# Early mixers: difference rows squared ahead of a step's maxima, one bias product for two

## The chip, the cores and the metric
One core of a Trainium2 chip runs the whole program. The metric is the device time of one execution in microseconds (us). The engines are TensorE (PE, with PEld for its weight loads), VectorE (DVE), ScalarE (ACT) and SyncE (SP), which issues the weight loads.

## The reference, cut to what matters
The program is a first block of two layers (hybrid mixer, dense or expert feed-forward, layer embedding) and a second block of two layers. The change is in the hybrid mixer of the first block, which runs once in each of its two layers. There, for 256 tokens:

```
qa, ka, va, qb, kb, vb, fb, qc, kc, vc, gc = split(xn @ w_in)
# difference attention: 8 softmax heads, 4 pairs
o   = causal_attention(qa, ka, va)
o_a = rmsnorm(o[:, :, 0] - lam * o[:, :, 1], subln_g) * (1 - lam_init)
# fox attention: 4 heads with a forget bias
log_f = log_sigmoid(fb + b_forget); cum = cumsum(log_f)
s[t, s'] = q[t] . k[s'] * scale + cum[t] - cum[s']     # then causal mask and softmax over s'
# retention: 4 heads, rotary on q and k, then group norm and silu gate
return concat(o_a, o_b, o_c) @ w_out
```

The term cum[t] is the same for every s' of a row, so the softmax over s' has the same value with or without it.

## The kernel before, in words
All work of an engine runs in one order written out by hand, and the engines wait for each other on counting semaphores. Weights come in pieces of 1 MB by SP into 7 raw slots. Each piece is rounded by ACT into a high part (`high`, 1.9 us) and DVE subtracts that for a low part (`low`, 2.3 us, L1684); PE multiplies with three products for each block (L676 to L678). Parts have three slots. `splits(done)` does the pieces up to three past the one named.

`attention1(l)` is written once for PE, once for ACT, once for DVE. It goes through steps i = 0 to 11, one head in each (`RUN1`): 0 to 7 are the difference heads, 8 to 11 the fox heads. On PE, step i does: `scores(i)`, the transposes `turn(i - 1)` (L774), the values product `values(i - 2)` (L783), and then half a projection of w_in (va, vfb, qkb, qkc, vgc, steps 0 to 9). In step 10 it transposes the rotated qc and kc instead; in steps 11 and 12 it does the retention scores (L883, L884) and values (L891 to L894). `scores` writes for two token tiles the product of q and k (L759), for a fox head the bias in two products against a one-hot column of the identity (L762 for cum[t], L763 for -cum[s']), and the causal mask (L765).

DVE in step i takes projected rows, then the row maxima of head i (`maxima`, L1852), then in steps 4, 6, 8 and 10 takes a finished pair of difference heads out of PSUM: reciprocal, scaling by lambda, two products (L1887 to L1891) into `ya` and `second`. Then the low parts of its piece. Step 6 has the chain of the forget gate, with two requests to ACT; step 8 the rotation of qc and kc (L2010 to L2015). At the end of step 10 DVE subtracts `second` from `ya` (L1914) and sums the squares (`squares_of`, L1991, L1992). After step 11 it requests the square root (`rstd_ask`, L1728), weighs two heads of retention scores (`weigh`, L1919), waits for the root (`rstd_answer`, L1733), applies root and gain (`gained`, L1985, L1987) and marks the rows ready (`mark`, L1711).

ACT in step i does the exponentials of head i (L1368) once their maxima are there, copies the turned probabilities of head i - 1 (L1378), and the high part of its piece. In step 10 it first copies the vgc rows (L1392, L1394), in step 11 first the transposed qc and kc (`take`, L1357), for which the retention scores wait. Its Sqrt for the difference rows (`serve_sqrt(8)`, L1284) comes after step 11. ACT changes its table of functions (ACT_TABLE_LOAD) between Exp and Sqrt; Copy needs none.

After this `mixed(l)` transposes the rows of all three parts (L647) and multiplies with w_out; these are the dense rows that begin at 158.68 us in layer 0.

Of the kernel before, what the change touches and what calls it, by code (L numbers as in the profile page):

```python
# [24 lines left out]
ALU = mybir.AluOpType  # L25
# [3 lines left out]
P = 128  # L29
# [9 lines left out]
HEADS4 = 4  # L39
# [81 lines left out]
def program(nc, io, out, cut=99):  # L121
    ctx = ExitStack()
    with ctx:
# [367 lines left out]
        def tok(i):  # L491
            return slice(i * P, (i + 1) * P)
# [142 lines left out]
        def _(pe):  # L635
# [113 lines left out]
            def scores(name, u, g):  # L749

                if g >= 2:
                    pe.wait_ge(att_exp, g - 1)
                q, k, _ = att_operands(name, u)
                for t, (c0, n) in enumerate(att_shape(name)[2]):
                    if name == "memory":
                        last = pe.matmul(bank[g % 2][:, c0:c0 + n], q[:, tok(t)], k[:, 0:n], start=True, stop=True)
                        continue
                    dst = bank[g % 2][:, c0:c0 + n]
                    pe.matmul(dst, q[:, tok(t)], k[:, 0:n], start=True, stop=False)  # L759
                    if name == "fox":  # L760
                        one = ident[0:HEADS4, u:u + 1]
                        pe.matmul(dst, fox[:, 2, tok(t)], one.to_broadcast([HEADS4, n]), start=False, stop=False)  # L762
                        pe.matmul(dst, one.to_broadcast([HEADS4, P]), fox[:, 3, 0:n], start=False, stop=False)  # L763

                    last = pe.matmul(dst[:, t * P:(t + 1) * P], ident_one[:, :], causal[:, :], start=False, stop=True)  # L765
                last.then_inc(att_scores, 1)
# [487 lines left out]
        def _(act):  # L1254
# [125 lines left out]
            def attention1(l):  # L1380

                first = att_first["diff", l]
                for i in range(len(RUN1) + 1):
                    if i == 2:
                        act.wait_ge(xn_ready, norm_no["mix", l] + 1)
                        for t in range(NT):
                            take(("va", l, t), v[:, t, 0:512], rst[:, t:t + 1])
                    if i == 10:
                        act.wait_ge(rotated, l + 1)
                        for t in range(NT):  # L1390
                            filled(act, ("vgc", l, t))
                            act.activation(sg[:, t, :], bank_of(("vgc", l, t))[:, 256:512], ACT.Copy,  # L1392
                                           scale=rst[:, t:t + 1])
                            act.activation(v[:, t, 768:1024], bank_of(("vgc", l, t))[:, 0:256], ACT.Copy,  # L1394
                                           scale=rst[:, t:t + 1]).then_inc(unit_act, 1)
                    if i == 11:
                        take(("qcT", l), flat(qT, 6, 2))
                        take(("kcT", l), flat(kT, 6, 2))
                    if i < len(RUN1):
                        exps(*RUN1[i], first + i)  # L1400
                    if i == 12:
                        serve_sqrt(8)
                    if i >= 1:
                        copy_turned(RUN1[i - 1][0], first + i - 1)
                    if i == 6:
                        serve(fox[:, 1, :], fox[:, 1, :], ACT.Exp, scale=-1.0)
                        serve(fox[:, 1, :], fox[:, 1, :], ACT.Ln, bias=1.0)
                    if 1 <= i <= 10:
                        splits(pieces_of[("va", "vfb", "qkb", "qkc", "vgc")[(i - 1) // 2], l][(i - 1) % 2])
                    if (l, i) == (0, 1):  # L1410
                        serve(stat[:, 1, 0:2 * LAYERS], stat[:, 0, 0:2 * LAYERS], ACT.Exp)
# [264 lines left out]
        def _(dve):  # L1676
# [178 lines left out]
            def attention1(l):  # L1855
# [4 lines left out]
                for i in range(len(RUN1)):  # L1860
                    if i == 4:
                        for t in range(NT):
                            key = ("vfb", l, t)
                            filled(dve, key)
                            dve.tensor_scalar(forget_rows[:, t, :], bank_of(key)[:, 256:260], rst[:, t:t + 1], None,
                                              ALU.mult)
                            dve.tensor_scalar(v[:, t, 512:768], bank_of(key)[:, 0:256], rst[:, t:t + 1], None,
                                              ALU.mult).then_inc(unit_dve, 1)
                    if i == 5:
                        take_scaled(("qkb", l, 0), qT[:, 4:6, :], 0.125)  # L1870
                    if i == 6:
                        key = ("forgetT", l)
                        filled(dve, key)
                        dve.tensor_scalar(fox[:, 0, :], bank_of(key)[0:HEADS4, 0:SEQ], bforget[:, l:l + 1], None,
                                          ALU.add).then_inc(unit_dve, 1)
                        take_scaled(("qkb", l, 1), kT[:, 4:6, :])
                    if i == 8:
                        for t in range(NT):
                            filled(dve, ("qkc", l, t))
                            dve.tensor_scalar(a1[:, t * G:(t + 1) * G], bank_of(("qkc", l, t))[:, :], rst[:, t:t + 1],  # L1880
                                              None, ALU.mult).then_inc(unit_dve, 1)
                    maxima(*RUN1[i], first + i)
                    if i in (4, 6, 8, 10):
                        hd = (i - 4) // 2
                        dve.wait_ge(att_pv, first + i - 2)
                        r = rinv[:, 4 * hd:4 * hd + 4]
                        link(dve.reciprocal(r, rowsum[:, 4 * hd:4 * hd + 4]))  # L1887
                        link(dve.tensor_scalar(r[:, 2:4], r[:, 2:4], lam[:, l:l + 1], None, ALU.mult))
                        o = bank[4 + hd % 2][:, :].rearrange("p (n t d) -> p n t d", n=2, t=NT)
                        dve.tensor_tensor(ya[:, :, hd, :], o[:, 0], per(r[:, 0:2], P), ALU.mult)  # L1890
                        dve.tensor_tensor(second[:, :, hd, :], o[:, 1], per(r[:, 2:4], P),  # L1891
                                          ALU.mult).then_inc(out_taken, 1)
                    if i == 6:
                        emptied(dve, ("forgetT", l))
                        link(dve.tensor_scalar(fox[:, 1, :], fox[:, 0, :], -1.0, None, ALU.mult))
                        ask(dve.tensor_tensor(fox[:, 1, :], fox[:, 1, :], fox[:, 0, :], ALU.max))
                        ask(dve.tensor_scalar(fox[:, 0, :], fox[:, 0, :], 0.0, None, ALU.min))
                        link(dve.tensor_tensor(fox[:, 0, :], fox[:, 0, :], fox[:, 1, :], ALU.subtract))
                        link(dve.memset(fox[:, 1, :], 1.0))
                        link(dve.tensor_tensor_scan(fox[:, 2, :], fox[:, 1, :], fox[:, 0, :], 0.0, ALU.mult, ALU.add))  # L1900
                        dve.tensor_scalar(fox[:, 3, :], fox[:, 2, :], -1.0, None, ALU.mult).then_inc(cum_ready, 1)
                    if 1 <= i <= 10:
                        splits(pieces_of[("va", "vfb", "qkb", "qkc", "vgc")[(i - 1) // 2], l][(i - 1) % 2])
                    if (l, i) == (0, 1):
                        setup_lambda()
                    if i == 8:
                        emptied(dve, ("qkc", l, 1))
                        rotate(a1[:, :].rearrange("p (t h n) -> p t h n", t=NT, h=8), 8, 0, 32, rot,
                               a2[:, :].rearrange("p (t h n) -> p t h n", t=NT, h=8),
                               [flat(qT, 6, 2), flat(kT, 6, 2),  # L1910
                                sg[:, :, :].rearrange("p t n -> p (t n)")]).then_inc(rotated, 1)
                    if i == 10:
                        dve.wait_ge(out_taken, out_use["diff", l, 3] + 1)
                        link(dve.tensor_tensor(ya, ya, second, ALU.subtract))  # L1914
                        squares_of(ya, 4, P)

                def weigh(u):
                    dve.wait_ge(ret_scores, HEADS4 * l + u + 1)
                    dve.tensor_tensor(ret_w[:, u, :], bank[6 + u % 2][:, 0:3 * P], decay[:, u, :],  # L1919
                                      ALU.mult).then_inc(ret_weights, 1)  # L1920

                rstd_ask(rinv[:, 0:8], 8, 1.0 / P)
                weigh(0)
                weigh(1)
                rstd_answer(8)
                link(gained(ya, 4, P, g_subln[:, l, :]))
                mark().then_inc(y_ready, 1)
                weigh(2)
                weigh(3)
                dve.wait_ge(att_pv, first + len(RUN1))  # L1930
# [585 lines left out]
```

## Time and profile before

| | |
|---|---|
| median of 3 runs | 2122.72 us (2120.93 to 2123.65) |
| the profiled execution's own time | 2124.18 us |
| its span, first to last instruction | 2122.4 us |
| busy share PE, DVE, ACT | 95%, 73%, 58% |
| granted clock of PE, mean | 0.970 |
| HBM traffic | 502 MB read, 237 GB/s over the span |

The busy share is a mean over stages that have different limits; the mixer's attention takes some 110 us in each of the two layers of 2122. A granted clock of 1.00 is 2.4 GHz, 0.50 is 1.2 GHz. In timelines the number in brackets is the time the engine stood idle before an instruction, with what ended it. Starts of following instructions of one engine can lie closer than their durations, since they overlap.

### The profile page before, as it was taken

What the parts mean: (1) busy time and instruction counts of PE and PEld (TensorE: products, weight loads), DVE (VectorE), ACT (ScalarE), POOL (GpSimd) and SP (SyncE); (2) the same over time, 40 slices, a digit from 0 to 9 for tenths busy, and PEclk for the clock granted to TensorE, in tenths of its full rate; (3) what the DMA queues carried; (4) which work ended last, traced back from release to release, by engine and by line L of the source; (5) the groups of instructions that cost most, each with busy time, mean ns of one, the idle gap of its engine ahead of it and who ended that gap; (6) DMA issues with size and microseconds to landing.
All of it is one profiled execution on the core that took longest, in us unless ns stands there. A gap on an engine that the chain in (4) does not pass through costs nothing.

```text
span 2122.4 us, 27418 instructions
## 1 busy us (share of the span) xinstructions
PE 2026.0 (95%) x10545; PEld 1711.3 (81%) x10545; DVE 1554.2 (73%) x1526; ACT 1234.5 (58%) x1300; POOL 0.2 (0%) x4
## 2 busy tenths in 40 slices
PE   5999999999899999999999999999988999999998
PEld 5878999887778888888888888888877887878886
DVE  4455555646579898988988898888885855866575
ACT  4434434644467777777777777777776545254532
POOL 0000000000000000000000000000000000000000
PEclk8978999999899999999999999999998999999999
DMA  8414555450479999999999999999975542335320
GB/s 269 161 60 144 183 195 190 130 178 1 168 256 378 334 370 345 358 375 329 375 331 368 347 355 377 328 374 334 369 275 176 179 145 74 126 137 194 119 71 29
DMA packets 242709, 504.47 MB, mean 238 GB/s; under 512 B 11321, under 2 KB 58681, under 8 KB 242617
## 3 DMA queue, kind: packets, MB, share of 16 engines
q1 hardware_dynamic: 242328, 503.10, 66.8%
q8 instruction: 63, 1.03, 0.2%
q14 instruction: 30, 0.24, 0.0%
q10 hardware_dynamic: 288, 0.11, 0.0%
HBM read 502.12 MB, written 1.05 MB: 237 GB/s over the span
## 4 chain that ended last, share of the span: by engine, by line
PE 86%; DVE 7%; ACT 3%; issue 2%; SPq 2%; DMA 0%; DVEq 0%; ACTq 0%
PE bank L676 25%; PE bank L678 25%; PE bank L677 25%; DVE low L1684 2%; PE bank L759 2%; PE bank L1086 1%; PE bank L783 1%; PE bank L1044 1%; ACT high L1264 1%; PE bank L647 1%; SPq L627 1%; PE bank L774 1%; PE bank L1173 1%; ACT high L1440 1%; SPq L591 1%
## 5 line engine op out<-in xcount | busy, mean ns | idle before, releaser
L2238 DVE TENSOR_TENSOR low<-raw,high 128x2048 fp32r<-128x2048 f32 x336 | 768.3, 2291 | 107.1 <-ACT high L1440 106.4
L1440 ACT ACTIVATE high<-raw 128x2048 fp32r<-128x2048 f32 x336 | 644.7, 1919 | 249.8 <-PE bank L678 247.9
L1684 DVE TENSOR_TENSOR low<-raw,high 128x2048 fp32r<-128x2048 f32 (+1 forms) x139 | 312.8, 2260 | 174.9 <-ACT high L1264 174.4
L1264 ACT ACTIVATE high<-raw 128x2048 fp32r<-128x2048 f32 (+1 forms) x139 | 262.9, 1896 | 178.4 <-PE bank L678 178.0
L676 PE MATMUL bank<-high,xg_hi 128*128 128x512 f32 x896 | 354.4, 396 | 2.5 <-DVE lone L2192 2.5
L678 PE MATMUL bank<-high,xg_lo 128*128 128x512 f32 x896 | 349.9, 391 | 0.0
L677 PE MATMUL bank<-low,xg_hi 128*128 128x512 f32 x896 | 349.3, 390 | 0.0
L676 PE MATMUL bank<-high,xT_hi 128*128 128x512 f32 (+1 forms) x576 | 230.4, 400 | 5.6 <-DVE xT_lo L1700 1.8
L677 PE MATMUL bank<-low,xT_hi 128*128 128x512 f32 (+1 forms) x576 | 223.9, 389 | 0.0
L678 PE MATMUL bank<-high,xT_lo 128*128 128x512 f32 (+1 forms) x576 | 223.8, 388 | 0.0
L676 PE MATMUL bank<-high,hT_hi 128*128 128x512 f32 x536 | 210.1, 392 | 0.0
L677 PE MATMUL bank<-low,hT_hi 128*128 128x512 f32 x536 | 208.7, 389 | 0.0
L678 PE MATMUL bank<-high,hT_lo 128*128 128x512 f32 x536 | 208.7, 389 | 0.0
L676 PE MATMUL bank<-xT_hi,high 128*128 128x256 f32 x672 | 195.1, 290 | 11.0 <-DVE low L1684 5.0
L676 PEld LDWEIGHTS bank<-high,xg_hi 128*128 128x128 f32 x896 | 168.7, 188 | 36.6 <-DVE lone L2192 2.8
L678 PEld LDWEIGHTS bank<-high,xg_lo 128*128 128x128 f32 x896 | 168.5, 188 | 36.0
L677 PEld LDWEIGHTS bank<-low,xg_hi 128*128 128x128 f32 x896 | 168.9, 188 | 33.8
L677 PE MATMUL bank<-xT_lo,high 128*128 128x256 f32 x672 | 193.4, 288 | 0.0
L678 PE MATMUL bank<-xT_hi,low 128*128 128x256 f32 x672 | 193.1, 287 | 0.0
L676 PEld LDWEIGHTS bank<-xT_hi,high 128*128 128x128 f32 x672 | 132.1, 197 | 13.0 <-issue 5.3
L676 PEld LDWEIGHTS bank<-high,xT_hi 128*128 128x128 f32 x576 | 110.4, 192 | 28.8 <-issue 2.2
L677 PEld LDWEIGHTS bank<-xT_lo,high 128*128 128x128 f32 x672 | 132.2, 197 | 0.4
(311 smaller groups left out, 2435.3 us busy)
## 6 DMA issues: line engine op xcount, KB each, us to landing
raw<-in_moe_w_gate SPq DMA_DIRECT2D x112, 1024.0 KB, 5.5
raw<-in_moe_w_up SPq DMA_DIRECT2D x112, 1024.0 KB, 5.6
raw<-in_moe_w_down SPq DMA_DIRECT2D x112, 1024.0 KB, 5.5
raw<-in_w_in SPq DMA_DIRECT2D x64, 1024.0 KB, 5.4
raw<-in_w_out SPq DMA_DIRECT2D x20, 1024.0 KB, 4.9
raw<-in_dense_w_gate SPq DMA_DIRECT2D x11, 1024.0 KB, 5.3
raw<-in_dense_w_up SPq DMA_DIRECT2D x11, 1024.0 KB, 5.4
raw<-in_dense_w_down SPq DMA_DIRECT2D x11, 1024.0 KB, 4.9
```

What stands on the lines that cost most here:

```text
L591: sp.dma_start(raw[:, slot, 0:k * n].rearrange("p (k n) -> p k n", k=k), src).then_inc(landed[slot], 16)
L627: sp.dma_start(dst, source).then_inc(consts_in, 16)
L647: last = pe.transpose(bank_of(key)[:, (k * NT + t) * P:(k * NT + t + 1) * P], rows[:, t, (2 * j + k) * P:(2 * j + k + 1) * P], ident[:, :])
L676: pe.matmul(dst, stationary[0], moving[0], start=start, stop=False)
L677: pe.matmul(dst, stationary[0], moving[1], start=False, stop=False)
L678: return pe.matmul(dst, stationary[1], moving[0], start=False, stop=stop)
L759: pe.matmul(dst, q[:, tok(t)], k[:, 0:n], start=True, stop=False)
L774: last = pe.transpose(bank[2 + g % 2][:, b * P:(b + 1) * P], probs[:, g % 2, b * P:(b + 1) * P], ident[:, :])
L1264: act.activation(high[:, slot, 0:k * n], raw[:, raw_slot[piece], 0:k * n], ACT.Copy).then_inc(high_done, 1)
L1440: act.activation(high[:, k % PARTS, :], raw[:, slot, :], ACT.Copy).then_inc(s["high"], 1)
L1684: dve.tensor_tensor(low[:, slot, 0:k * n], src, high[:, slot, 0:k * n].bitcast(F32), ALU.subtract).then_inc(low_done, 1)
L2238: dve.tensor_tensor(low[:, k % PARTS, :], raw[:, at0 + k % slots, :], high[:, k % PARTS, :].bitcast(F32), ALU.subtract).then_inc(s["low"], 1)
```

## The change
Five edits, all in `scores` and the two `attention1` of ACT and DVE. The product of cum[t] (L762) is left out. On DVE the maxima of each step go behind the take-out of a pair (steps 4, 6, 8, 10); in step 10 the subtraction, the squares and the request for the root go ahead of the maxima, and the answer, root, gain and mark right behind them, where all of these stood after the low part of step 10 or after step 11. The low part of step 10 goes to step 11, behind its maxima. On ACT the Sqrt goes from step 12 to step 10, between the vgc copies and the exponentials.

```
@@ scores (PE)
                     pe.matmul(dst, q[:, tok(t)], k[:, 0:n], start=True, stop=False)
                     if name == "fox":
                         one = ident[0:HEADS4, u:u + 1]
-                        pe.matmul(dst, fox[:, 2, tok(t)], one.to_broadcast([HEADS4, n]), start=False, stop=False)
                         pe.matmul(dst, one.to_broadcast([HEADS4, P]), fox[:, 3, 0:n], start=False, stop=False)
@@ attention1 (ACT)
                             act.activation(v[:, t, 768:1024], bank_of(("vgc", l, t))[:, 0:256], ACT.Copy,
                                            scale=rst[:, t:t + 1]).then_inc(unit_act, 1)
+                        serve_sqrt(8)
                     if i == 11:
                         take(("qcT", l), flat(qT, 6, 2))
                         take(("kcT", l), flat(kT, 6, 2))
                     if i < len(RUN1):
                         exps(*RUN1[i], first + i)
-                    if i == 12:
-                        serve_sqrt(8)
@@ attention1 (DVE)
-                    maxima(*RUN1[i], first + i)
                     if i in (4, 6, 8, 10):
                         hd = (i - 4) // 2
...
                                           ALU.mult).then_inc(out_taken, 1)
+                    if i == 10:
+                        dve.wait_ge(out_taken, out_use["diff", l, 3] + 1)
+                        link(dve.tensor_tensor(ya, ya, second, ALU.subtract))
+                        squares_of(ya, 4, P)
+                        rstd_ask(rinv[:, 0:8], 8, 1.0 / P)
+                    maxima(*RUN1[i], first + i)
+                    if i == 10:
+                        rstd_answer(8)
+                        link(gained(ya, 4, P, g_subln[:, l, :]))
+                        mark().then_inc(y_ready, 1)
...
-                    if 1 <= i <= 10:
+                    if 1 <= i <= 9:
                         splits(pieces_of[("va", "vfb", "qkb", "qkc", "vgc")[(i - 1) // 2], l][(i - 1) % 2])
+                    if i == 11:
+                        splits(pieces_of["vgc", l][1])
...
-                    if i == 10:
-                        dve.wait_ge(out_taken, out_use["diff", l, 3] + 1)
-                        link(dve.tensor_tensor(ya, ya, second, ALU.subtract))
-                        squares_of(ya, 4, P)
...
-                rstd_ask(rinv[:, 0:8], 8, 1.0 / P)
                 weigh(0)
                 weigh(1)
-                rstd_answer(8)
-                link(gained(ya, 4, P, g_subln[:, l, :]))
-                mark().then_inc(y_ready, 1)
                 weigh(2)
                 weigh(3)
```

## Rows read from the trace of the kernel before

**Rows 1.** The page, part 4: shares of the span in the chain that ended last, by engine
```profile
PE 86%; DVE 7%; ACT 3%; issue 2%; SPq 2%; DMA 0%; DVEq 0%; ACTq 0%
```

**Rows 2.** PE's waits, layer 0, 50 to 165 us: us in total, times, longest
```profile
PE bank L774 <- ACT probs L1368: 4.0, 1, 4.0
```

**Rows 3.** The same of layer 1, 430 to 550 us
```profile
PE bank L774 <- ACT probs L1368: 4.2, 1, 4.2
```

**Rows 4.** The chain in order of time, layer 0: start, us, what
```profile
138.39 2.29 DVE low L1684
140.68 1.14 DVE yf L1914
...
141.85 1.24 DVE scr L1991
...
143.10 1.23 DVE rinv L1992
...
144.36 0.63 DVE negmax L1852 x2
...
145.98 0.90 PE bank L774 x3
```

**Rows 5.** Timeline of PE, layer 0: start, us, instruction
```profile
131.85 0.48 PE L762 MATMUL bank<-ident,yf 4*128 4x128 f32 x2
132.18 0.38 PE L763 MATMUL bank<-yf,ident 4*128 4x128 f32 x2
...
133.28 0.70 PE L762 MATMUL bank<-ident,yf 4*128 4x256 f32 x2
133.81 0.59 PE L763 MATMUL bank<-yf,ident 4*128 4x256 f32 x2
...
140.34 1.18 PE L883 MATMUL bank<-qT,kT 64*128 64x256 f32 x4
...
158.68 0.76 PE L676 MATMUL bank<-high,xT_hi 128*128 128x512 f32 x1 [0.73 <-issue]
```

**Rows 6.** Timeline of DVE, layer 0; in brackets the idle time before and its releaser
```profile
97.08 0.17 DVE L1887 RECIPROCAL rinv<-rowsum 128x4 f32<-128x4 f32 x1
...
98.22 0.27 DVE L1895 TENSOR_SCALAR yf<-yf 4x256 f32<-4x256 f32 x1
...
113.90 0.62 DVE L1852 TENSOR_REDUCE negmax<-bank 128x1 f32<-128x128 f32 x2 [1.34 <-PE bank L765]
...
127.66 2.29 DVE L1684 TENSOR_TENSOR low<-raw,high 128x2048 fp32r<-128x2048 f32 x1 [3.17 <-ACT high L1264]
```

**Rows 7.** Timeline of ACT, layer 0, step 10
```profile
135.26 0.37 ACT L1368 ACTIVATE probs<-bank,negmax 128x128 f32<-128x128 f32 x1 [2.08 <-DVE negmax L1852]
...
138.71 0.61 ACT L1357 ACTIVATE kT<-bank 128x512 f32<-128x512 f32 x1
```

**Rows 8.** Timeline of ACT, second attention, around its Sqrt
```profile
1729.72 1.28 ACT L1284 ACT_TABLE_LOAD   x1
...
1731.24 1.28 ACT L1368 ACT_TABLE_LOAD   x1
```

**Rows 9.** Timelines of DVE and PE, layer 1
```profile
499.81 0.62 DVE L1852 TENSOR_REDUCE negmax<-bank 128x1 f32<-128x128 f32 x2 [1.68 <-PE bank L765]
...
510.59 0.62 DVE L1852 TENSOR_REDUCE negmax<-bank 128x1 f32<-128x128 f32 x2 [0.72 <-PE bank L765]
514.38 2.29 DVE L1684 TENSOR_TENSOR low<-raw,high 128x2048 fp32r<-128x2048 f32 x1 [3.17 <-ACT high L1264]
...
525.84 0.98 PE L883 MATMUL bank<-qT,kT 64*128 64x256 f32 x4
...
531.49 0.90 PE L774 MATMUL bank<-ident,probs 128*128 128x128 f32 x3 [4.24 <-ACT probs L1368]
```

**Rows 10.** Stretches: length, busy PE, PEld, DVE, ACT, POOL; PEclk, DMA share, GB/s
```profile
123.50:126.50 3.00, 3.00 (x13) 2.71 (x12) 0.99 (x3) 1.98 (x6) 0.00 (x0) 0.50 0.37 125
...
140.50:164.00 23.50, 18.73 (x76) 16.27 (x77) 16.52 (x32) 5.82 (x14) 0.00 (x0) 0.50 0.00 0
```

## The prediction

> **What bounds the kernel now.** I read four views. First the page's chain of waits: TensorE (PE) holds 86% of the chain that ended last [rows 1], so a microsecond counts where PE idles for another engine, or where PE itself has less to do with nothing else late. Second, PE's waits in the two attention stretches: each has one large wait, 4.0 us in layer 0 and 4.2 us in layer 1, of the last fox head's transposes (L774) for its exponentials [rows 2, 3]. Third, the chain in order of time shows what stands in that wait: the low part of a weight piece (L1684), subtraction, squares and their sum (L1914, L1991, L1992), then the maxima of the last step (L1852), then exponentials [rows 4]. The difference rows, 3.7 us of VectorE (DVE) work, stand ahead of maxima that PE waits for. Fourth, the timelines of PE, DVE and ScalarE (ACT) [rows 5 to 7, 9], from which the new order can be laid out. I number the steps i = 0 to 11 as the code does; steps 8 to 11 are the fox heads.
>
> **The bias product (L762).** It goes 16 times, 8 in each layer. By starts, one for the first token tile takes 132.18 - 131.85 = 0.33 us of PE and one for the second 133.81 - 133.28 = 0.53 us [rows 5], so a head saves 0.86 us, a layer 3.4 us, both 6.9 us. Whether it shortens anything depends on what is late next.
>
> **The out-take block (L1887 to L1891) now stands ahead of the maxima of steps 4, 6, 8 and 10.** From its start to the next instruction it takes 98.22 - 97.08 = 1.14 us [rows 6]. The values product it waits for is that of head i - 3, which PE does in step i - 1 ahead of that step's projection, so the wait is over by then. In step 8 DVE idled 1.34 us in layer 0 and 1.68 us in layer 1 ahead of the maxima [rows 6, 9]: the block fits. In steps 4 and 6 it delays the maxima by up to 1.1 us; PE asks for those exponentials only a step later, some 5 us or more after the scores, and the fox gate chain of step 6 stood behind the same block before, so it gets at most some 0.15 us later. I take 0 on PE for these three steps and -0.1 us on the DVE chain that leaves step 8 of layer 0, because scores (8) are ready 0.86 us earlier, and DVE, not PE, is then the later. Step 9 follows at DVE's own pace, since the rotation fills it: in layer 0, low part (9) starts at 127.66 - 0.1 and the next DVE instruction can start 2.21 us later (its 2.29 us less an overlap of 0.08), so DVE is free at F = 129.77. In layer 1 the maxima of steps 8 and 9 did wait for PE, 1.68 us (of which the block uses 1.14) and 0.72 us [rows 9]; both shrink as scores come earlier, so this chain gains 0.54 + 0.72 = 1.25 us: F = 514.38 - 1.25 + 2.21 = 515.34.
>
> **Step 10, DVE.** From F: block with its link 1.25 us (1.14 plus 0.1 for the last instruction's end), then L1914, L1991, L1992 at 1.25 to 1.26 each by their starts [rows 4], 3.77: the request for the square root is issued at F + 5.0. Scores (10) are ready before that, so the maxima follow at once and end at F + 5.7. The subtraction used to be behind the low part of step 10; that low part moves behind the maxima of step 11, and no one is near needing it: its piece belongs to the output projection.
>
> **Step 10, ACT.** ACT now waits in its queue for that request, and exponentials (10), copy (9), the high part and the two copies of qc and kc are queued behind it. The Sqrt needs another activation table than Exp. The second attention has just this order: a table load of 1.28 us at 1729.72, the Sqrt, and the load back at 1731.24, 1.52 us after the first [rows 8]. I take the first load as put ahead of the wait, where ACT has 3 us of idle; it costs nothing there (without that cover, 1.28 us a layer). The load back is bare: a load and a Sqrt, 1.52 us by the starts of rows 8. With 0.2 from request to Sqrt, exponentials (10) start at F + 6.72. Before they started at 135.26, and kc's copy ended at 138.71 + 0.61 = 139.32, 4.06 us later [rows 7]; the instructions between are the same. So kc is there at F + 10.8, and the retention scores (L883), which wait for it, start at 140.57 instead of 140.34 in layer 0 and at 526.15 instead of 525.84 in layer 1 [rows 5, 9]. **PE's saving is thus all given back at this point**: it idles about 1.6 us ahead of transposes (10) and 2.2 us ahead of L883.
>
> The Trainium skill ("ScalarE: Activation LUTs", What ACT_TABLE_LOAD costs) puts a switch of table at 1.28 us plus a drain of 1.38 us. By the skill the load back would end 1.38 us later and the sum below would be 2.8 us smaller. The trace disagrees: 1.52 us hold the load of 1.28 us and the Sqrt, with no room for a drain [rows 8].
>
> **Step 11 and after.** L883 and L884 take 1.6 us (140.34 to the start of the idle, 145.98 - 4.04) [rows 2, 4, 5]. The gain rows (L1985, L1987) and the mark are done by F + 8.5, maxima (11) right behind, exponentials (11) on ACT at F + 10.8 to 11.7: all ahead of PE. Transposes (11) then start at 142.17, where they started at 145.98: **3.8 us earlier**; in layer 1 at 527.75 against 531.49 [rows 9]: **3.75 us**. The first retention weights are due 1.9 us later; the moved low part lets DVE go at F + 12.1, in time. From there to the output projection PE was busy throughout. The square root of the retention norm needs its own table load now; ACT idled 4 us ahead of it, so it is covered.
>
> PE's clock was at half (1.2 GHz, granted 0.50) from 140.5 to 164.0 us in layer 0 [rows 10], and for as long in layer 1; it fell before the wait of 4 us began, while PE did small products, and rose 5.3 us into the dense rows, which began at 158.68 [rows 5]. I leave that stretch as it is, merely 3.8 us shorter. The short fall inside the fox steps (123.5 to 126.5 [rows 10]) may go or stay; since DVE sets the pace there, it does not move the end. What is gained carries to the end: the expert stage waits for PE, not for transfers, and loads start when pieces are used.
>
> **Sum.** 3.8 + 3.75 = 7.5 us. The profiled execution took 2124.18 us, which makes 2116.7; the median of the runs is 1.46 us lower, so I forecast 2115.2 us. A measurement of this kernel can tell about 0.2%, 4.2 us, from no change.
>
> **Rivals.**
> *PE sets the pace after all.* If my DVE and ACT chain is too long, the two waits (8.2 us) and all products (6.9 us) go: 15.1 us, 2107.6. For it: PE's 86%. Against it: kc's copy cannot come before the square root in ACT's order. 10%.
> *The switch of table holds ACT a load's length longer*: the first load bare too, or ACT at a standstill around the second, 1.28 us more a layer, 2117.8. For it: in rows 8 the request had come before the load, so they don't show on which side of a pending wait it stands. Against it: their load back is bare of anything else. 14%. The Trainium skill's drain (same section) would be such a standstill.
> *The blocks of steps 4, 6 and 8 add up* instead of sinking into idle time: 3.4 us a layer on F, which leaves 0.4 us: 2122.0, no difference. Against it the idle time ahead of the maxima in rows 6 and 9. 12%.
> *The clock stays down* (the slower side). Place: the rows of the output projection. With the new idle pieces among small products PE could come to the dense rows needing longer to be given 2.4 GHz. Each microsecond of full speed work done at half costs one more; from 3.75 us of such work a layer the gain is gone, and if 8.6 us of the rows behind 164.0 were done at half, the time would be 2115.2 + 17.2 = 2132.4. Against it: the clock came back 5.3 us into the dense rows, which began at 158.68 [rows 5, 10] and are unchanged. 6%.
> The forecast itself has 58%.
>
> **Numbers.** The forecast's own range, with runs spread over 2.7 us and the clock's rise some 1.5 us earlier or later, is 2112 to 2118.5. The range of 8 in 10 takes in the bare load and most of the adding up: 2111 to 2121. The chance of faster by over 0.2% (below 2118.5): 0.58 less a little, 0.10 and over half of 0.14, 0.74; within 0.2%: 0.20; slower: 0.06.
>
> **What would show it.** PE's waits should show the 4 us wait on exponentials (11) gone, and in its place some 1.6 us ahead of transposes (10) and 2.2 us ahead of the retention scores, waiting for kc's copy, in each layer. ACT should show a load, Sqrt and load between its vgc copies and exponentials (10). L762's group should be gone with the other bias product left at 32 records. DVE should run from F without idle to maxima (10). I am wrong if the retention scores start over 1 us earlier or later against the end of the projections than laid out, or if the low clock outlasts the first 6 us of the dense rows.

## The result and the profile after

| | before | changed |
|---|---|---|
| median of the runs on one chip (4 each) | 2123.18 us (2120.93 to 2128.11) | 2109.07 us (2107.55 to 2113.32) |
| ratio, 95% interval | | 0.9939 [0.9919, 0.9959] |
| profiled execution: time, span, mean granted clock | 2124.18, 2122.4 us, 0.970 | 2113.32, 2111.5 us, 0.971 |
| PE's wait ahead of transposes (11), layer 0, layer 1 | 4.0, 4.2 us | 0, 0 us |
| forecast | | 2115.2 us (2111 to 2121) |

The sign is right. The time lies 6.1 us below the forecast and 1.9 us below the range. Of the runs behind the table of experiments, three took 4017, 6585 and 7007 us and are left out of every median, mean and ratio. The profile after, first the page's shares of the chain that ended last, against [rows 1]:

```profile
PE 81%; DVE 10%; ACT 5%; issue 2%; SPq 2%; DMA 0%; DVEq 0%; ACTq 0%
```

PE lost five points to DVE and ACT, on which more of the chain now lies. PE's waits in layer 0 (100 to 150 us), against [rows 2]; columns are us in total, times, longest:

```profile
PE bank L885 <- ACT kT L1359: 0.6, 1, 0.6
```

and in layer 1 (480 to 600 us), against [rows 3]:

```profile
PE bank L776 <- ACT probs L1370: 1.9, 1, 1.9
PE bank L885 <- ACT kT L1359: 1.1, 1, 1.1
```

The wait of 4 us is gone, and two smaller ones stand a step earlier, where the prediction had them. The chain in order of time, layer 0, against [rows 4] (start, us, what):

```profile
128.64 2.29 DVE low L1685
...
132.11 1.24 DVE yf L1895
...
133.37 1.24 DVE scr L1995
...
134.63 1.23 DVE rinv L1996
...
135.88 0.18 DVE stat L1729
...
136.31 1.28 ACT L1370
...
137.61 0.02 ACT probs L1370
...
141.19 0.49 ACT kT L1359
...
141.72 1.23 PE bank L885 x4
```

It is now one chain from the low piece to the retention scores: difference rows, request, load back, exponentials (10), kcT. From low (9) to exponentials (10) it takes 137.61 - 128.64 = 8.97 us; the working had 2.21 + 6.72 = 8.93. ACT's timeline beside it, against [rows 7, 8]:

```profile
131.68 1.28 ACT L1286 ACT_TABLE_LOAD   x1
136.09 0.21 ACT L1286 ACTIVATE stat<-stat 128x8 f32<-128x8 f32 x1 [3.12 <-DVE stat L1729]
136.31 1.28 ACT L1370 ACT_TABLE_LOAD   x1
137.61 0.37 ACT L1370 ACTIVATE probs<-bank,negmax 128x128 f32<-128x128 f32 x1
...
141.06 0.61 ACT L1359 ACTIVATE kT<-bank 128x512 f32<-128x512 f32 x1
```

The first load stands ahead of the pending wait (it ends at 132.96, the Sqrt goes at 136.09), so it is hidden; the load back is bare, with exponentials 0.02 us behind it. PE's timeline, layer 0, against [rows 5]:

```profile
130.35 0.48 PE L765 MATMUL bank<-yf,ident 4*128 4x128 f32 x2
130.76 0.23 PE L767 MATMUL bank<-causal,ident_one 128*128 128x128 bf16 x1
130.92 0.70 PE L759 MATMUL bank<-kT,qT 64*128 64x256 f32 x2
131.55 0.69 PE L765 MATMUL bank<-yf,ident 4*128 4x256 f32 x2
132.17 0.23 PE L767 MATMUL bank<-causal,ident_one 128*128 128x128 bf16 x1
...
143.31 0.90 PE L776 MATMUL bank<-ident,probs 128*128 128x128 f32 x3
```

A token tile's bias by starts now takes 130.76 - 130.35 = 0.41 us and 132.17 - 131.55 = 0.62 us. Transposes (11) start 143.31 - 128.64 = 14.67 us behind low (9), where before it was 145.98 - 127.66 = 18.32 us [rows 4, 6]: 3.65 us less behind that point, and the point itself comes earlier.

**Where the time went.** Against scores (4), transposes (11) start 4.1 us earlier in each layer, 8.2 us together, forecast 7.5. Of the 10.9 us between the two spans another 2.65 us come from the start of the dense stage, where the kernel before had TensorE at half clock (first line) and the changed one did not (second):

```profile
189.00:195.00 6.00, 5.92 (x27) 0.50 1.07 369
```

```profile
189.00:195.00 6.00, 6.00 (x53) 1.00 1.08 373
```

(Stretch, length, PE's busy time and instructions, PEclk, DMA share, GB/s.) The changed kernel's first step began 1.45 us late, and the rest, 1.5 us, is small shifts. The cause of that half clock is open. In the mixers' ends the low clock stayed. Windows of the changed kernel, against [rows 10], first its tail of layer 0, then the stretch in which the kernel before has its short fall:

```profile
133.20:159.60 26.40, 25.09 (x101) 20.68 (x101) 16.88 (x30) 9.83 (x21) 0.00 (x0) 0.50 0.00 1
```

```profile
122.00:127.00 5.00, 5.00 (x27) 1.00 0.68 210
```

The long fall lasts 26.4 us (23.5 before), the short one is gone. The long fall began at 133.2 us, while PE was busy, and ahead of its only wait in this stretch (141.1 to 141.7 us).

### The profile page after: what moved, and what is told of

It is laid out like the page before. It is cut to its first block, busy times and chain, and to the rows that moved or that the text cites. A ratio compares the mean times of both kernels' runs of the same rounds, so it can differ in the third digit from the quotient of the medians.

```text
span 2111.5 us, 27356 instructions
## 1 busy us (share of the span) xinstructions
PE 2019.1 (96%) x10513; PEld 1703.5 (81%) x10513; DVE 1553.0 (74%) x1526; ACT 1239.0 (59%) x1304; POOL 0.2 (0%) x4
## 4 chain that ended last, share of the span: by engine, by line
PE 81%; DVE 10%; ACT 5%; issue 2%; SPq 2%; DMA 0%; DVEq 0%; ACTq 0%
PE bank L676 24%; PE bank L678 24%; PE bank L677 24%; DVE low L1685 3%; ACT high L1266 2%; PE bank L1088 1%; PE bank L1046 1%; PE bank L785 1%; PE bank L759 1%; PE bank L647 1%; SPq L627 1%; ACT probs L1370 1%; PE bank L1175 1%; ACT high L1441 1%; SPq L591 1%
```

## Experiments

PE's tail below is the time from transposes (11) to the last turned rows of y, layer 0; "wait" is PE's wait ahead of transposes (11) alone, so a kernel with 0 there can still wait elsewhere. Mean clock is the mean over a kernel's runs. The ratio is to the runs of the kernel before on the same chip, which had, in the four comparisons, medians of 2118.27 (the first four rows), 2118.08 (late root, late root with step 10 only, copy, before again), 2117.01 (late root again, product back and the delays) and 2116.78 us (the last row), and mean clocks of 0.9713 or 0.9714.

| kernel | median us | ratio, 95% interval | mean clock | wait L0, L1 | tail |
|---|---|---|---|---|---|
| changed, again | 2108.43 | 0.9952 [0.9937, 0.9968] | 0.9742 | 0, 0 | 26.1 |
| product alone | 2113.18 | 0.9973 [0.9964, 0.9982] | 0.9736 | 5.4, 5.4 | 25.5 |
| order alone | 2115.38 | 0.9992 [0.9977, 1.0007] | 0.9711 | 0, 0 | 24.2 |
| step 10 only | 2112.04 | 0.9956 [0.9939, 0.9973] | 0.9736 | 0, 0 | 26.3 |
| late root | 2089.38 | 0.9861 [0.9840, 0.9882] | 0.9835 | 0, 0 | 20.5 |
| late root, again | 2091.92 | 0.9891 [0.9863, 0.9919] | 0.9805 | 0, 0 | 20.5 |
| late root, step 10 only | 2095.27 | 0.9904 [0.9871, 0.9936] | 0.9787 | 0, 0 | 20.5 |
| copy for the root | 2107.83 | 0.9943 [0.9924, 0.9962] | 0.9740 | 0, 0 | 26.2 |
| before, again | 2120.34 | 1.0007 [0.9994, 1.0020] | 0.9702 | 4.2, 4.2 | 26.9 |
| late root, product back | 2115.86 | 0.9984 [0.9970, 0.9999] | 0.9713 | 0, 0 | 26.5 |
| late root, delay of one | 2108.78 | 0.9959 [0.9945, 0.9974] | 0.9735 | 2.5, 2.5 | 27.0 |
| late root, delay of two | 2110.04 | 0.9964 [0.9951, 0.9977] | 0.9749 | 5.0, 5.0 | 25.6 |
| product and late root | 2102.49 | 0.9923 [0.9897, 0.9950] | 0.9775 | 1.3, 1.3 | 25.4 |

**The changed kernel again**, on the chip of the next three.

> The changed kernel itself, unchanged, run again to see how steady its gain is and how it goes with the granted clock. What the two traces show at matched places: the stretch from the fourth scores to the output projection is 4.1 us shorter in each layer, 8.2 us in all, where 7.5 were forecast; the rest of the 10.9 us between the profiled executions is half-clock time elsewhere. Theory A (the rest is chance in when the clock falls): 8 to 9 us faster than before once executions of the same mean clock are compared, and 8 to 14 as medians fall. Theory B (the change itself makes the clock fall less often): again 12 to 14 us faster, and the mean clock of all its executions 0.002 or more above the kernel before. Theory C (layout or another lasting cause outside the mixers): 12 to 14 us faster at equal clock.

2108.43 us, ratio 0.9952: 9.8 us faster on this chip. That size is between theory A's 8 to 9 and the 12 to 14 of B and C, and the interval reaches from 6.8 to 13.3 us; the mean clock lies 0.0029 above the kernel before, the sign that theory B names. Its trace shows the waits of layer 0 whole:

```profile
PE bank L776 <- ACT probs L1370: 1.9, 1, 1.9
PE bank L885 <- ACT kT L1359: 1.8, 1, 1.8
```

3.7 us; the prediction had 1.6 + 2.2 = 3.8. In the first trace PE's clock had already fallen at 133.2, its small products took longer, and they covered 3.1 us of the same waits; the retention scores started at the same point of DVE's chain both times. Layer 1 has 1.9 + 1.1 = 3.0 us in both traces: there the clock fell during the first wait, and the slower products behind it covered 0.7 us of the second.

**The product alone**: the kernel before without the query's product.

```
-                        pe.matmul(dst, fox[:, 2, tok(t)], one.to_broadcast([HEADS4, n]), start=False, stop=False)
```

> The kernel before with the product of cum[t] (L762) left out and nothing moved. Theory A (the chain through VectorE and ScalarE sets the pace in step 9 and 10, as laid out): in the order of before, scores (10) are late for VectorE by 4.65 us in layer 0 and 3.44 us in layer 1, so all three products ahead of it count, 3 x 0.86 = 2.6 us a layer, and the fourth is swallowed by the 4 us wait: 5.2 us faster, the waits of TensorE on the last exponentials stay at 4.0 us plus 0.86. Theory B (fewer falls of the clock): the short fall in a fox step, 3 us at half in each layer, is gone too: 7 to 8.5 us faster with a higher mean clock. Rival (additive): 6.9 us and the waits shrink by none.

5.1 us faster, by the interval 3.8 to 7.6, so the time alone can't tell theory A's 5.2 from the additive rival's 6.9. The wait ahead of transposes (11) grew from 4.0 to 5.4 us, so PE's own saving is partly given back to it, as a chain paced by DVE makes it. Yet the trace gains 3.6 us a layer from scores (4) to transposes (11), 7.2 us in all, nearer to theory B. The starts of scores (8), (9) and (10) stand 9.54 and 11.17 us apart before, 8.88 and 8.87 us here: 0.66 us a step for the product, and 1.6 us for a short fall of the clock that is not there any more.

**The order alone**: the changed kernel with the query's product back.

```
                         one = ident[0:HEADS4, u:u + 1]
+                        pe.matmul(dst, fox[:, 2, tok(t)], one.to_broadcast([HEADS4, n]), start=False, stop=False)
```

> The changed kernel with the product of cum[t] put back, so only the order of VectorE and ScalarE differs from before. Theory A: the retention scores start at F + 10.8 with F = 129.95 and 516.67, that is 0.4 and 1.6 us later than before, and the last transposes 3.6 and 2.5 us earlier: 6.1 us faster. With the product alone at 5.2 the two don't add up to more than the change because the product's time is lost in front of the copy of kc: sum 11.3 against 8.2. Rival (additive): change minus product, 13 - 6.9 = 6 us, and product alone 6.9, so that the sum is the change. Theory B: as A, and the mean clock like that of before, 0.970, as the long fox steps are back.

2.9 us faster by the medians, 0.9992 [0.9977, 1.0007]: not told from no change, where theory A had 6.1 us. PE waits for no other engine in the mixer's end of either layer, and still the retention scores of layer 0 start 1.7 us later than before, counted from scores (4), and those of layer 1 3.6 us later. Transposes (11) start 2.4 and 0.4 us earlier, where theory A had 3.6 and 2.5. Two windows of this kernel show why:

```profile
117.00:122.00 5.00, 5.00 (x18) 0.68 0.22 74
...
127.00:132.00 5.00, 5.00 (x22) 0.66 0.00 1
```

Both steps, 8 to 9 and 9 to 10, take 11.14 us; the kernel before has one such fall. In layer 1 the long fall comes early, at some 513 us:

```profile
510.00:520.00 10.00, 10.00 (x41) 0.64 0.00 0
```

(the kernel before: 1.00 in this window, and at half only from some 526 us). The wait was exchanged for work at half clock. So product and order are worth 5.1 and 2.9 us alone and 9.8 together by the medians, each good to some 2 to 3 us.

**Step 10 only**: the changed kernel with the maxima ahead of the scaling rows in steps 4, 6 and 8.

```
+                    if i != 10:
+                        maxima(*RUN1[i], first + i)
                     if i in (4, 6, 8, 10):
...
-                    maxima(*RUN1[i], first + i)
                     if i == 10:
+                        maxima(*RUN1[i], first + i)
```

> The changed kernel with the maxima of steps 4, 6 and 8 ahead of the take-out of a pair again; step 10 stays as changed. Theory A (those three moves cost and bring nothing on TensorE): equal to the changed kernel within 1 us; VectorE's step 8 starts its maxima as soon as scores (8) are there, up to 0.9 us earlier, so the last transposes come up to 0.9 us earlier in each layer if the chain through VectorE is the bound: 0 to 1.8 us faster than the changed kernel. Rival (the moves ahead matter by themselves): slower than the changed kernel by over 2 us.

The intervals overlap almost wholly, 0.9956 against 0.9952; in the traces its transposes (11) come 0.2 us a layer earlier against scores (4). So in the traces the blocks of steps 4, 6 and 8 cost 0.2 us a layer, which the times can't show.

**The late root.** The waits of 1.9 and 1.8 us are the price of asking for the root ahead of exponentials (10). This kernel keeps the scaling rows first, but lets the difference rows follow the maxima, answers the root after two retention weighings, and has ACT serve it in step 12.

```
+                    maxima(*RUN1[i], first + i)
                     if i == 10:
                         dve.wait_ge(out_taken, out_use["diff", l, 3] + 1)
                         link(dve.tensor_tensor(ya, ya, second, ALU.subtract))
                         squares_of(ya, 4, P)
                         rstd_ask(rinv[:, 0:8], 8, 1.0 / P)
-                    maxima(*RUN1[i], first + i)
-                    if i == 10:
-                        rstd_answer(8)
-                        link(gained(ya, 4, P, g_subln[:, l, :]))
-                        mark().then_inc(y_ready, 1)
...
                 weigh(1)
+                rstd_answer(8)
+                link(gained(ya, 4, P, g_subln[:, l, :]))
+                mark().then_inc(y_ready, 1)
                 weigh(2)
```

> The changed kernel with the two pieces of its step 10 put apart: the scaling rows still run ahead of step 10's maxima, but subtraction, squares and sums come behind those maxima, and the root is asked for there and answered only between the second and third retention weighing, with the vector engine's last low piece after step 11's maxima; the scalar engine serves the root in step 12 again. Theory A (in the changed kernel step 10's exponentials wait for 3.7 us of difference rows, for the root and for two table loads): without these exponentials start some 5 us earlier after the block, the copy of kcT stands at step 10's scores + 7.0 us instead of + 11.1, retention's first scores at + 7.6 instead of + 11.8, and the transposes of step 11 at + 9.2 instead of + 13.4 us: 4.2 us a layer, some 8 us in all, so about 2101 us where the changed kernel has 2109, ratio to the kernel before about 0.992. Rival (the difference rows only change places: they come late for the turned rows y at the end of the mixer, as in the kernel before, so TensorE waits there instead): the transposes of step 11 come earlier by 4 us and the first turned y row does not; the time stays within 1 us of the changed kernel.

2089.38 us: theory A had 2101, and the gain over the changed kernel is 19 us instead of 8 (the two ran on different chips; their ratios, 0.9861 and 0.9952, say the same). PE's timeline in layer 0:

```profile
129.07 0.49 PE L759 MATMUL bank<-kT,qT 64*128 64x128 f32 x2
...
136.65 0.71 PE L885 MATMUL bank<-qT,kT 64*128 64x256 f32 x4
...
137.57 0.55 PE L776 MATMUL bank<-ident,probs 128*128 128x128 f32 x3
```

Scores (10) to the retention scores: 7.58 us, to transposes (11): 8.50 us (9.2 expected, 13.4 in the changed kernel). That is 4.9 us a layer. Another 5.8 us a layer stand behind transposes (11): the tail takes 20.5 us instead of 26.3, because the clock no longer falls (130 to 165 us, the changed kernel 0.61):

```profile
130.00:165.00 35.00, 32.84 (x190) 1.00 0.00 1
```

The changed kernel's transposes of 0.90 us take 0.55 us here. Neither theory had this part. PE is not without waits here. The retention weights come late twice in each layer, and the clock stays at 1.00 through it:

```profile
PE bank L893 <- DVE ret_w L1924: 1.0, 2, 0.6
```

**The late root with step 10 only**: steps 4, 6 and 8 as in the kernel before.

> The kernel with the late root, and in steps 4, 6 and 8 the maxima ahead of the scaling rows as in the kernel before; only step 10 keeps the rows first. Theory A: as the step-10-only kernel stood to the changed one in their traces, 0.2 us a layer earlier, 0.4 us in all, which the times can't tell; the same time as the kernel with the late root. Rival (the order in steps 4, 6 and 8 matters by the clock, which falls where TensorE works on little): over 1 us to either side.

Its trace is that of the late root to 0.1 us up to the dense stage, but its six runs reach from 2088.2 to 2110.2 us, with mean clocks from 0.986 down to 0.971. The median lies 5.9 us above the late root's on this chip and 3.4 us above its repeat; the ratios' intervals overlap with both, so neither theory A nor the rival is settled by the times.

**A copy in place of the root** (no table changes in step 10; the kernel leaves the square root out).

```
-                        serve_sqrt(8)
+                        serve(stat[:, 1, 0:8], stat[:, 0, 0:8], ACT.Copy)
```

> The changed kernel, where the scalar engine answers the request of step 10 with a copy instead of the root (this leaves the root out of the normalised rows of the first mixer, in both layers), so neither its table load nor the load back to the exponentials' table takes place. Theory A (the load back, 1.28 us, stands between the answer and step 10's exponentials; the load ahead is hidden in the wait): step 10's exponentials start some 1.0 to 1.3 us earlier, TensorE's waits of 0.6 us (layer 0) and 1.1 us (layer 1) on kcT go, 1.7 us in all, up to 2.5 us if the later scores of layer 1 also move up. Rival (nothing waits on it: TensorE has other work): below 0.5 us.

ACT's timeline, layer 0:

```profile
134.12 0.21 ACT L1286 ACTIVATE stat<-stat 128x8 f32<-128x8 f32 x1 [4.45 <-DVE stat L1729]
134.64 0.37 ACT L1370 ACTIVATE probs<-bank,negmax 128x128 f32<-128x128 f32 x1 [0.32 <-DVE negmax L1853]
```

Exponentials (10) start 0.52 us after the answer instead of 1.52; the maxima are then the later by 0.32. From scores (10) to transposes (11) it takes 12.42 us instead of 13.38 and 13.37: 0.95 us a layer, 1.9 us together, theory A's size. The waits for kcT, which theory A had go, stay at 1.9 and 1.1 us; it is the wait of 1.9 us ahead of transposes (10) that shrinks to 1.0. The times, 2107.83 against 2108.43, on different chips, can't show it.

**The kernel before again**, as a kernel of its own.

> The kernel before, unchanged, against itself: how far apart two medians of it come, and a second trace of it. Theory A (the three runs that the prediction started from lay high, and most of the miss comes from there): its own median is 2117.5 to 2119.5 us, not 2122.7, and the two stand at 1.000 within 0.001. Theory B (the short falls of TensorE's clock in the mixers' last steps belong to this order of instructions): its trace shows one of them, some 1.6 us long, between the scores of step 9 and of step 10 in each layer again. Rival to B: they fall in other steps, or in none.

1.0007 [0.9994, 1.0020], but 2.3 us apart in the medians: 2120.34 us (12 runs) and 2118.08 us (17). Theory A's bound of 2119.5 us is passed; its second half, 1.000 within 0.001, holds. All five later medians of this kernel do lie 2.4 to 5.9 us below the 2122.72 us of the first three runs. The second trace has one short fall in each layer too, in layer 0 a step earlier, in layer 1 again between scores (8) and (9); so the rival to theory B holds for layer 0:

```profile
112.00:117.00 5.00, 5.00 (x21) 0.66 0.64 206
```

It also has the half clock at the start of the dense stage. Which step it falls in differs between the traces; that it falls once is the same in both traces and both layers.

**The product back, and two delays**, all from the late root: what holds the clock?

```
+                        pe.matmul(dst, fox[:, 2, tok(t)], one.to_broadcast([HEADS4, n]), start=False, stop=False)
```

> The kernel with the late root, with the query's part of the forget bias added by its own product again in each fox head: the kernel before but for the order of step 10 and of the root. Theory A (what brought 20 us below the changed kernel is TensorE's clock, which stays at full in the end of the mixers when step 11's transposes don't wait; the product isn't needed for that): 4 x 0.66 = 2.6 us a layer back, and a short fall of the clock of 1.6 us a layer in the steps 8 to 10 as in the traces of the kernel before; 6 to 9 us above the kernel with the late root, 2095 to 2098 us, ratio to before 0.988 to 0.990. Rival (the product belongs to what holds the clock): the clock falls again at the end of the mixers, 12 us more, 2107 to 2111 us.

24 us slower than the late root on the same chip, for 5.3 us of products: the rival's direction, and 5 us beyond its range. PE waits for no other engine in its tail, and its clock falls at some 134 us all the same:

```profile
130.00:135.00 5.00, 5.00 (x24) 0.90 0.00 0
135.00:140.00 5.00, 5.00 (x22) 0.50 0.00 0
```

The delays do squares and sums of the difference rows twice, or three times, ahead of maxima (11):

```
-                        squares_of(ya, 4, P)
+                        for again in range(2):
+                            squares_of(ya, 4, P)
```

> The kernel with the late root, with squares and sums of the difference rows done twice over (the second time changes nothing), ahead of step 11's maxima: 2.5 us of work more on the vector engine at a place where its exponentials have some 0.15 us to spare, so TensorE's transposes of step 11 wait about 2.3 us in each layer. Theory A (a wait there lets the clock fall until the projection after the mixer is well under way): 2.3 us of waiting and some 6 us of half clock a layer, 16 us in all, about 2105 us. Rival (a wait costs itself alone): 4.6 us, about 2094 us.

> The same with squares and sums done three times over: 5.0 us more on the vector engine, a wait of about 4.8 us a layer. Theory A: 4.8 us of waiting and 6 us of half clock a layer, about 2111 us; the step from no delay to one (16 us) is larger than the step from one to two (5 us). Rival (a wait costs itself alone): 9.6 us, about 2099 us, both steps the same.

With one, the wait is 2.5 us in each layer:

```profile
PE bank L776 <- ACT probs L1370: 2.5, 1, 2.5
```

```profile
135.00:140.00 5.00, 2.50 (x24) 1.00 0.00 0
140.00:145.00 5.00, 4.45 (x24) 0.60 0.01 3
```

and the time 2108.78, 16.9 us above the late root of the same chip (16 expected; 4.6 by the rival). PE idles at full clock, and the fall comes behind the wait. With two, the wait is 5.0 us, the time 2110.04: 1.3 us more, not 5. Theory A's shape holds, its second step is too large; the tail shrinks from 27.0 to 25.6 us, and the two intervals overlap. Here the fall comes inside the wait, which ends at 143.69 us:

```profile
140.00:145.00 5.00, 1.31 (x7) 0.72 0.00 0
```

**The late root again**, beside these three.

> The kernel with the late root once more, on the chip of its three variants: 2089 us and a mean clock of 0.983 again if its gain belongs to the kernel; a spread as wide as that of its sister with step 10 alone (2088 to 2110 us) if it is a chance of each execution whether the clock holds in both mixers.

2091.92 us, and the trace the same in the tail; its six runs reach from 2082.8 to 2102.5 us, clocks from 0.986 to 0.974. Both expectations are half right: the gain belongs to the kernel, and how much of it a run gets is partly chance.

**Product and late root, without the change's order of the scaling rows.**

```
+                    maxima(*RUN1[i], first + i)
                     if i in (4, 6, 8, 10):
...
-                    maxima(*RUN1[i], first + i)
                     if i == 10:
```

> The kernel with the late root, with the scaling rows behind the maxima again in steps 4, 6, 8 and 10, as in the kernel before: of the change only the product is left, and the late root stands on it. By the trace of the kernel with the late root, the 1.2 us of scaling rows then stand between step 10's maxima and the difference rows, step 11's maxima come 1.2 us later, and step 11's transposes wait about 1.1 us in each layer, between none (late root) and 2.5 us (delay of one). Theory A (the order of the scaling rows is worth nothing but this wait, and the clock holds through it): 2.2 us above the kernel with the late root, 2091 to 2096 us. Rival (a wait of 1.1 us is enough for the clock to fall): 2104 to 2109 us, as with the delay of one; then the change's order is what makes the gain of the late root possible.

PE waits 1.3 us in each layer:

```profile
PE bank L776 <- ACT probs L1370: 1.3, 1, 1.3
```

```profile
135.00:140.00 5.00, 3.22 (x27) 1.00 0.00 0
140.00:145.00 5.00, 4.97 (x24) 0.53 0.01 3
```

and the clock falls in this trace in both layers. The median is 2102.49 us, the runs from 2093.9 to 2110.1: between the two forecasts, neither holds. The spread suggests that a wait of 1.3 us makes the fall likelier, not certain; only one execution has a trace. The scaling rows' place is worth 7 to 13 us here by the ratios (0.9923 against the late root's 0.9891 and 0.9861, each on its own chip); its interval overlaps with that of the late root's repeat, so the size is rough.

## Why the prediction was off

**Right.** The chain on DVE and ACT, to 0.04 us from low (9) to exponentials (10); the first table load hidden and the load back bare, with no drain; the waits' new places and their sum (3.7 against 3.8 us in layer 0 of the second trace; 3.0 us in layer 1 of both, where the clock fell in between); the moved low piece free; the blocks of steps 4, 6 and 8 sunk into idle time, but for 0.2 us a layer; PE's own saving given back: 4.1 us a layer where 3.8 and 3.75 were laid out.

**The steps that failed.**

1. *"the median of the runs is 1.46 us lower, so I forecast 2115.2 us"*. The base of three runs lay high: later medians of the same kernel are 2116.8 to 2120.3 us. A forecast of -7.5 us is a ratio of 0.9965, outside the first comparison's [0.9919, 0.9959] and just inside the second's [0.9937, 0.9968]. From the base of that second chip, 2118.27 us, it reads 2110.8 us, 2.3 us above what was measured there. So 4.5 us of the 6.1 us is the base, and the range took this spread too lightly. Whether the first runs lay high by chance, or something lasting about that chip raised the kernel before alone, no run tells: the changed kernel had 2109.07 us there and 2108.43 us on the second. The first comparison's 14.1 us between the medians contain that high base too; 9.8 us is the better figure for the change.
2. *"a head saves 0.86 us"*. It is 0.66: the kept product lost its overlap, 0.41 and 0.62 us by starts where they were (with the two together) 0.33 and 0.53 us for the removed one alone. The sum went by DVE's chain, so this changed nothing in it.
3. *"The short fall inside the fox steps may go or stay; since DVE sets the pace there, it does not move the end."* It went: in all 22 mixers traced without the product (11 traces of 9 kernels) scores (8), (9) and (10) stand 8.87 or 8.88 us apart, while of the eight traced with it six have falls in these steps. And it did move the end a little: low (9) starts 50.10 us behind scores (4) instead of 50.57 in layer 0, and 50.02 instead of 51.67 in layer 1, 0.47 and 1.65 us earlier, where 0.1 and 1.25 were laid out. That is about the 0.7 us that the two layers gained over the forecast. Which part of it the fall gave, and which the product, was not taken apart.
4. *"I leave that stretch as it is"*. For this change it held, as the change left waits of 3.0 to 3.7 us a layer. This stretch held the larger prize, some 6 us a layer, and no case priced it. The half clock at the start of the dense stage, 2.65 us in both traces of the kernel before and in neither of the changed one, was not seen either; kernels with and without the product show it, so its cause stays open, and with it some 1.6 us of the miss.

**The rivals.** PE setting the pace (2107.6) came out close in time but not in mechanism: 3.0 to 3.7 us of waits a layer remained. The table switch and the adding up are refuted by the timelines. The clock staying down (the slower side) did not occur; its opposite was what mattered. The order alone came nearest to it: there the clock's falls ate over 3 us of the 6 us expected by the traces.

## What to carry to other kernels

Where TensorE runs small products, a wait can cost more than its length (in the late root 2.5 us in each of two layers cost 16.9 us), and taking part of a wait out can be worth little: here 4.0 and 4.2 us of waits were exchanged for 3.7 and 3.0 us, and only the kernel with no wait for another engine above 0.6 us left (2089.4 us) got the clock's 6 us a layer. Taking the waits out is not enough by itself: with the query's product back the same kernel fell to half clock with no wait for another engine in its tail (2115.9 us). Whether it is the kind of that product or merely its 0.66 us a head was not tested. Read the granted clock window by window around each wait before pricing it, and price "hardly any wait" as a case of its own. Take the base of a forecast from more than three runs where the change is worth less than their spread.

## What was not expected of the hardware

- TensorE's granted clock through the mixer's end (130 to 165 us) is 0.66 before, 0.61 and 0.71 in the two traces of the changed kernel, 0.76 with one delay, and 1.00 in the late root; with the query's product back it falls at 134 us with no wait for another engine. Once down, it stayed at half (1.2 GHz) for 26.4 us in layer 0 of the changed kernel's first trace.
- In the kernel with one delay the clock is 1.00 while PE idles and 0.60 in the 5 us behind: the fall comes after the wait, so the wait itself looks harmless. With two delays it falls inside the longer wait, and in the kernel before it had already fallen at some 140.5 us [rows 10], when the wait of 4 us began only at 141.9 us.
- Executions of one kernel differ by the clock's falls: 2082.8 us at a mean of 0.986 and 2102.5 at 0.974 for the late root, some 1.6 us for each 0.001.
